# Even and odd tokens in the Hyena transforms, and the order of the work around them

## The reference

```
h   = modulated rmsnorm(x)                                  # 256 x 1024
u   = short_conv(h @ w_hyena)                               # 256 x 1536, cut into v, g1, g2 of 512
z   = v
for o in 0, 1:                                              # long convolution by FFT, then a gate
    z = g[o] * irfft(rfft(z, 512) * rfft(filter[o], 512))[:256]
q, k, v = h @ w_qkv (k and v also of 256 memory rows)       # 4 heads, rotary positions on q and k
a   = softmax(q1 k1) v - lambda * softmax(q2 k2) v          # differential attention, 8 (head, tile) pairs
x   = x + w_out(gates of h) . (z, norm(a));  x = x + swiglu(x)
```

## Time and profile before

| | |
|---|---|
| median of 3 runs | 1320.81 us (1318.42 to 1324.71) |
| profiled execution, its own time | 1318.56 us |
| its span | 1316.8 us |
| TensorE (PE) busy | 1278.4 us, 97% of the span |
| VectorE (DVE) busy | 695.5 us, 53% |
| ScalarE (ACT) busy | 500.4 us, 38% |
| granted TensorE clock, mean over the span | 0.999 |
| DMA | 363.15 MB, mean 276 GB/s |

### The profile page before, as it was taken

How to read it: one execution, slowest core, us unless ns; L and a number is a source line. 1 busy time by engine, 2 the same in 40 slices (tenths; PEclk the granted TensorE clock), 3 DMA queues, 4 the chain that set the end, 5 groups by cost and what they waited for, 6 DMA issues and landing times.

```text
span 1316.8 us, 17834 instructions
## 1 busy us (share of the span) xinstructions
PE 1278.4 (97%) x7078; PEld 892.6 (68%) x7078; DVE 695.5 (53%) x1192; ACT 500.4 (38%) x766; POOL 77.8 (6%) x86
## 2 busy tenths in 40 slices
PE   8999999999999999999999999999999999999998
PEld 7987886976675454444444444449957687799986
DVE  5675678667564322223222222257875877755552
ACT  5556574345332111111111111146414685744442
POOL 5740200100000000000000000000000000000000
PEclk9999999999999999999999999999999999999999
DMA  9654747959855999999999999995505235655540
GB/s 351 232 189 151 240 144 286 353 186 333 312 203 217 401 429 428 427 429 426 428 428 428 428 427 427 426 389 185 179 13 210 110 137 159 194 165 180 190 160 33
DMA packets 102100, 363.15 MB, mean 276 GB/s; under 512 B 4114, under 2 KB 28949, under 8 KB 89920
## 3 DMA queue, kind: packets, MB, share of 16 engines
q1 hardware_dynamic: 98656, 352.86, 69.1%
q0 software_dynamic: 3168, 9.06, 2.1%
q10 hardware_dynamic: 192, 0.06, 0.0%
HBM read 360.91 MB, written 1.05 MB: 275 GB/s over the span
## 4 chain that ended last, share of the span: by engine, by line
PE 86%; DVE 6%; ACT 4%; issue 2%; DMA 1%; ACTq 0%; DVEq 0%
PE bank L532 38%; PE bank L925 16%; PE bank L943 8%; PE bank L902 5%; PE bank L1290 5%; PE bank L972 3%; DVE ring_parts L1338 2%; PE bank L854 1%; PE bank L933 1%; PE bank L1093 1%; PE bank L1082 1%; ACT ring_parts L2163 1%; PE bank L586 1%; DMA ring<-in_w_xkv 1%; PE bank L621 1%
## 5 line engine op out<-in xcount | busy, mean ns | idle before, releaser
L2163 ACT ACTIVATE ring_parts<-ring 128x1024 fp32r<-128x1024 f32 x234 | 242.6, 1057 | 226.5 <-PE bank L532 198.7
L1338 DVE TENSOR_TENSOR ring_parts<-ring,ring_parts 128x1024 fp32r<-128x1024 f32 x214 | 257.0, 1223 | 129.8 <-ACT ring_parts L2163 126.9
L532 PE MATMUL bank<-ring_parts,arena_parts 128*128 128x512 f32 x1056 | 271.8, 392 | 3.6 <-ACT ring_parts L2163 1.5
L532 PEld LDWEIGHTS bank<-ring_parts,arena_parts 128*128 128x128 f32 x1056 | 196.5, 188 | 48.7 <-ACT ring_parts L2163 2.9
L532 PE MATMUL bank<-arena_parts,ring_parts 128*128 128x256 f32 x1504 | 198.0, 284 | 2.2 <-DVE ring_parts L1338 1.2
L925 PE MATMUL bank<-ring,arena 128*64 128x512 f32 x432 | 190.6, 594 | 9.1 <-issue 9.1
L926 PE MATMUL bank<-ring,arena 128*64 128x512 f32 x448 | 198.0, 595 | 0.0
L532 PEld LDWEIGHTS bank<-arena_parts,ring_parts 128*128 128x128 f32 x1504 | 190.1, 192 | 4.1 <-issue 2.7
L925 PEld LDWEIGHTS bank<-ring,arena 128*64 128x64 f32 x432 | 57.4, 137 | 127.6 <-issue 127.6
L532 PE MATMUL bank<-ring_parts 128*128 128x512 f32 (+1 forms) x624 | 117.1, 345 | 2.1 <-DVE ring_parts L1338 1.2
L532 PEld LDWEIGHTS bank<-ring_parts 128*128 128x128 f32 x624 | 96.6, 190 | 22.0 <-issue 7.1
(11 more groups left out here) (390 smaller groups left out, 1416.2 us busy)
## 6 DMA issues: line engine op xcount, KB each, us to landing
ring<-in_w SPq DMA_DIRECT2D x81, 2048.0 KB, 21.5
ring<-in_w_in SPq DMA_DIRECT2D x27, 2048.0 KB, 9.6
flank<-in_w SPq DMA_DIRECT2D x13, 2048.0 KB, 22.1
ring<-in_w_ada SPq DMA_DIRECT2D x12, 2048.0 KB, 8.7
ring<-in_w_ffn_gate SPq DMA_DIRECT2D x11, 1024.0 KB, 5.4
ring<-in_w_ffn_up SPq DMA_DIRECT2D x11, 1024.0 KB, 8.0
ring<-in_w_ffn_down SPq DMA_DIRECT2D x5, 2048.0 KB, 7.7
ring<-in_w_xkv SPq DMA_DIRECT2D x4, 2048.0 KB, 16.4
```

Source lines behind the costliest of these rows:

```text
L532: mm = pe.matmul(ps[:, o:o + width], *pair, start=(o == 0 and kk == 0 and ha + hw == 0), stop=(kk == kn - 1 and (ha, hw) == terms[-1] and ...
L1338: dve.tensor_tensor(low, src, high, ALU.subtract).then_inc(low_ready, 1)
L2163: act.activation(high, src, ACT.Copy).then_inc(high_ready, 1)
```

## The change

Tokens are taken as even and odd ones. The frequencies come in pairs whose tables differ in nothing but the sign of the odd tokens' part, so half of the products suffice and VectorE makes the two halves by a sum and a difference. This holds for the spectra, the forward transforms and, with sum and difference ahead of the product, for the way back. What is done on which engine:

- TensorE: `transformed(o)` is 4 fp32 products of 128x512 instead of 8, `convolved(o)` 4 instead of 8, the spectra 8 instead of 16 in all. Transposes and tables read every second token.
- ScalarE: a new `even_halves(o)` copies two of the four U banks to SBUF, since VectorE's sums read one operand from PSUM and one from SBUF.
- VectorE: `filtered(o)` is 4 operations on 512 elements from PSUM, then 6 on 1024 and 4 on 512 in SBUF, instead of 12 on 512. `spectra_of_halves` adds two operations of 1024 elements in each of the expert steps 2 and 3. `rotate(Kall)` is cut into its two tiles, with `split_low(2)` between; `rotate(Q)` still stands between the two orders.
- Fillers: `transformed(0)` follows the transposes directly, all four quarters of Q stand between it and `convolved(0)`, and all four of V between `transformed(1)` and `convolved(1)`. From there each filler is taken one place earlier: quarter 0 of p7 stands ahead of the attention loop, and its iterations use quarters 1 to 3 of p7, p8, and quarter 0 of p9. The calls of `split_low`, `split_high` and `gate_columns` follow.
- The input table of transforms is laid out anew, with the same number of DMAs.

The diff, cut to its core and its indentation by eight (edits of other tables' layouts are left out):

```
 add(name, *[((lambda u, i=i: u[:, 512 * i:512 * i + 512].rearrange("p (k n) -> p k n", k=2)),
-             w["dft"][i].rearrange("(k p) n -> p k n", p=P)) for i in range(4)])
+             w["dft"][i].rearrange("(p k) n -> p k n", k=2)) for i in range(2)],
+    *[((lambda u, i=i: u[:, 512 * i:512 * i + N]), w["dft"][i][0:P, :]) for i in (2, 3)])
 ...
+evens, Yother = [actT[:].rearrange("p k n -> p (k n)")[:, D * i:D * (i + 1)].rearrange("p (i n) -> p i n", i=2) for i in range(2)]
...
         ps = take(f"spec{o}{part}{f}", bank)
-        for t in range(NT):
-            mm = pe.matmul(ps[:], tab[:, t, f * P:(f + 1) * P], hF[:, t, (2 * o + part) * 512:(2 * o + part + 1) * 512],
-                           start=(t == 0), stop=(t == 1))
-        give(f"spec{o}{part}{f}", mm)
+        give(f"spec{o}{part}{f}", pe.matmul(ps[:], tab[:, f, 0:P], hF[:, f, (2 * o + part) * 512:(2 * o + part + 1) * 512],
+                                            start=True, stop=True))
...
             for j in range(4):
-                mm = pe.transpose(ps[:, j * P:(j + 1) * P], uT[:, 4 * i + j, t * P:(t + 1) * P], ident[:])
+                mm = pe.transpose(ps[:, j * P:(j + 1) * P], uT[:, 4 * i + j, t:N:2], ident[:])
...
     def transformed(o):
-        fcos, fsin = unit("dftB", 2, N, 0), unit("dftB", 2, N, 512)
-        if o:
-            pe.wait_ge(s["Z_ready"], 2)
-        else:
-            emptied(pe, "utok00", "utok10")
-        for part, tab in enumerate((fcos, fsin)):
-            for f in range(2):
-                ps = bank(f"U{o}{part}{f}")
-                for t in range(NT):
-                    mm = pe.matmul(ps[:], tab[:, t, f * P:(f + 1) * P], (Z if o else UT)[:, t, 0:DHY], start=(t == 0), stop=(t == 1))
-                give(f"U{o}{part}{f}", mm)
+        tabs = unit("dftB", 2, N, 0), unit("dftB", 2, N, 512)
+        for parity in range(2):
+            if o:
+                pe.wait_ge(s["Z_ready"], parity + 1)
+            else:
+                emptied(pe, f"utok{parity}0")
+            for part in range(2):
+                ps = bank(f"U{o}{part}{parity}")
+                give(f"U{o}{part}{parity}", pe.matmul(ps[:], tabs[part][:, parity, 0:P], (Z if o else UT)[:, parity, 0:DHY],
+                                                      start=True, stop=True))
     def convolved(o):
-        icos, isin = unit("dftB", 2, N, 1024), unit("dftB", 2, N, 1536)
-        pe.wait_ge(s["Y_ready"], 4 * (o + 1))
-        for t in range(NT):
-            ps = bank(f"conv{o}{t}")
-            n = 0
-            for tab, Y in ((icos, Yre), (isin, Yim)):
-                for f in range(2):
-                    mm = pe.matmul(ps[:], tab[:, f, t * P:(t + 1) * P], Y[:, f, :], start=(n == 0), stop=(n == 3))
-                    n += 1
-            give(f"conv{o}{t}", mm)
+        tabs = unit("dftB", 1, N, 1024), unit("dftB", 1, N, 1536)
+        for parity in range(2):
+            pe.wait_ge(s["Y_ready"], 2 * o + parity + 1)
+            ps = bank(f"conv{o}{parity}")
+            for part, Y in enumerate((Yre, Yother)):
+                mm = pe.matmul(ps[:], tabs[part][:, 0, parity:N:2], Y[:, parity, :], start=(part == 0), stop=(part == 1))
+            give(f"conv{o}{parity}", mm)
         if o:
             used("dftB")
-    filler("p3", 0, 1)
     transformed(0)
-    filler("p3", 2, 3)
+    filler("p3", 0, 1, 2, 3)
     convolved(0)
-    filler("p5", 0)
     transformed(1)
-    filler("p5", 1, 2, 3)
+    filler("p5", 0, 1, 2, 3)
     convolved(1)
     filler("p6", 0, 1)
     pe.wait_ge(s["Z_ready"], 4)
...
         for h in range(H):
             mm = pe.transpose(ps[:, h * P:(h + 1) * P], Q[:, t, h * P:(h + 1) * P], ident[:])
         give(f"qT{t}", mm)
-    filler("p6", 2)
+    filler("p6", 2, 3)
     for t in range(4):
         ps = bank(f"kT{t}")
         for h in range(H):
             mm = pe.transpose(ps[:, h * P:(h + 1) * P], Kall[:, t, h * P:(h + 1) * P], ident[:])
         give(f"kT{t}", mm)
-    filler("p6", 3)
+    filler("p7", 0)
     emptied(pe, *jobs_of("qT", 2), *jobs_of("kT", 4))
     def dscores(n):
...
     for n in range(H * NT):
         if n + 1 < H * NT:
             dscores(n + 1)
-        filler(("p7", "p8")[n // 4], n % 4)
+        filler(("p7", "p8", "p9")[(n + 1) // 4], (n + 1) % 4)
         turned_weights(n)
         if n:
             attended(n - 1)
-    filler("p9", 0)
+    filler("p9", 1)
     attended(H * NT - 1)
-    filler("p9", 1, 2, 3)
+    filler("p9", 2, 3)
     UNIT_END[SLOT["hT"]] = PART_END[-1]
     for q in range(4):
         place = 4 * hT_place + q
...
         dve.scalar_tensor_tensor(out=yB[1][:, c], in0=PS[4 + half][:], scalar=slot_gate, in1=yB[0][:, c],
                                  op0=ALU.mult, op1=ALU.subtract).then_inc(moe[f"low{half}"], 1)
+    def spectra_of_halves(o):
+        emptied(dve, *[f"spec{o}{part}{f}" for part in range(2) for f in range(2)])
+        even, odd = spectra[:, 0, o], spectra[:, 1, o]
+        did(dve.tensor_tensor(even, even, odd, ALU.add))
+        did(dve.scalar_tensor_tensor(out=odd, in0=odd, scalar=-2.0, in1=even, op0=ALU.mult, op1=ALU.add))
     def acc(n):
         for half in range(2):
             for t in range(NT):
...
             xg(n + 1, 1)
         low(n, 0)
         low(n, 1)
+        if n in (2, 3):
+            spectra_of_halves(n - 2)
         if not before:
             acc(n)
...
         did(dve.tensor_copy(UT[:, t, 0:512], ps[:]), free(f"utok{t}0"))
     emptied(dve, "p4_0", "p4_1")
     dve.wait_ge(s["rope_in"], 32)
-    rotate(Kall)
+    rotate(Kall, (0,))
     split_low(2)
     def filtered(o):
         hr, hi = spectra[:, :, o, 0, :], spectra[:, :, o, 1, :]
-        for f in range(2):
-            ur = full(dve, f"U{o}0{f}")
-            did(dve.tensor_tensor(Yre[:, f, :], ur[:], hr[:, f, :], ALU.mult), hold=False)
-            did(dve.tensor_tensor(Yim[:, f, :], ur[:], hi[:, f, :], ALU.mult), free(f"U{o}0{f}"), hold=False)
-        for f in range(2):
-            ui = full(dve, f"U{o}1{f}")
-            did(dve.tensor_tensor(Ytmp[:, f, :], ui[:], hi[:, f, :], ALU.mult))
-            did(dve.tensor_tensor(Yre[:, f, :], Yre[:, f, :], Ytmp[:, f, :], ALU.subtract), s["Y_ready"])
-            did(dve.tensor_tensor(Ytmp[:, f, :], ui[:], hr[:, f, :], ALU.mult), free(f"U{o}1{f}"))
-            did(dve.tensor_tensor(Yim[:, f, :], Yim[:, f, :], Ytmp[:, f, :], ALU.add), s["Y_ready"])
-    def gated_on(o):
+        for part, X in enumerate((Yre, Yim)):
+            emptied(dve, f"U{o}{part}0")
+            odd = full(dve, f"U{o}{part}1")
+            did(dve.tensor_tensor(X[:, 0, :], evens[:, part, :], odd[:], ALU.add), hold=False)
+            did(dve.tensor_tensor(X[:, 1, :], evens[:, part, :], odd[:], ALU.subtract), free(f"U{o}{part}1"))
+        did(dve.tensor_tensor(Ytmp, Yre, hr, ALU.mult), hold=False)
+        did(dve.tensor_tensor(Yother, Yim, hi, ALU.mult))
+        did(dve.tensor_tensor(Ytmp, Ytmp, Yother, ALU.subtract))
+        did(dve.tensor_tensor(Yother, Yre, hi, ALU.mult))
+        did(dve.tensor_tensor(Yim, Yim, hr, ALU.mult), hold=False)
+        did(dve.tensor_tensor(Yre[:, 0, :], Ytmp[:, 0, :], Ytmp[:, 1, :], ALU.add), hold=False)
+        did(dve.tensor_tensor(Yre[:, 1, :], Ytmp[:, 0, :], Ytmp[:, 1, :], ALU.subtract))
+        did(dve.tensor_tensor(Yim, Yim, Yother, ALU.add))
+        did(dve.tensor_tensor(Yother[:, 0, :], Yim[:, 0, :], Yim[:, 1, :], ALU.add), s["Y_ready"])
+        did(dve.tensor_tensor(Yother[:, 1, :], Yim[:, 0, :], Yim[:, 1, :], ALU.subtract), s["Y_ready"])
+    def gated_on(o, t):
+        emptied(dve, f"utok{t}{o + 1}")
+        ps = full(dve, f"conv{o}{t}")
+        did(dve.tensor_tensor(Z[:, t, :], ps[:], UT[:, t, (o + 1) * 512:(o + 2) * 512], ALU.mult), free(f"conv{o}{t}"))
+        dve.sem_inc(s["Z_ready"], 1)
+    rotate(Kall, (1,))
+    for o in range(2):
+        filtered(o)
         for t in range(NT):
-            emptied(dve, f"utok{t}{o + 1}")
-            ps = full(dve, f"conv{o}{t}")
-            did(dve.tensor_tensor(Z[:, t, :], ps[:], UT[:, t, (o + 1) * 512:(o + 2) * 512], ALU.mult), free(f"conv{o}{t}"))
-            dve.sem_inc(s["Z_ready"], 1)
-    filtered(0)
-    split_low(1)
-    gated_on(0)
-    split_low(3)
-    emptied(dve, "p3_0", "p3_1")
-    rotate(Q)
-    filtered(1)
-    split_low(2)
-    gated_on(1)
+            split_low(1)
+            gated_on(o, t)
+        if o == 0:
+            split_low(2)
+            emptied(dve, "p3_0", "p3_1")
+            rotate(Q)
     split_low(1)
     def tile_places(k):
         return [(slice(None), slice(0, 4), slice(t * P, (t + 1) * P)) for t in range(NT)]
-    split_banks(["zT0", "zT1"], zT_parts, tile_places(4))
-    split_low(2)
+    split_banks(["zT0", "zT1"], zT_parts, [(slice(None), slice(0, 4), slice(t, N, 2)) for t in range(NT)])
+    split_low(3)
     def columns(n):
         o = 8 + 8 * (n % 2)
...
     evicted("p5c", Vall, NT)
     split_high(4 * 3 + 2)
     evicted("p4", Kall)
+    def even_halves(o):
```

(14 more changed lines are left out.)

8 lines of the change are left out of this document (4 added, 4 removed).

## The result

The changed kernel takes 1345.07 us (median of 4 runs, 1343.07 to 1345.68), the kernel before 1321.1 us in the same comparison. The ratio is 1.0177, with a 95% interval of 1.015 to 1.0204: slower by 24 us, where 14 were forecast and the range ended at 1341. The profiled execution took 1344.96 us, its span 1343.2.

A forecast was written before the change was run, and what follows sets the result against it. TensorE, 97% busy, was taken as the bound, with the experts' stream DMA-bound. Spectra -2.3, loop with Hyena +14.8 and clock +1.7 made +14.2: 1332.8 on the profiled execution, 1335.0 us as median, range 1327 to 1341.

The forecast's parts named there:

- Part 1, the spectra: Ahead of the experts: halved spectra let the expert weight stream start earlier, taken as 2.3 us gained.
- That is 1.8 at the first place freed and 2.6 at the second: Gain in us when TensorE's expert products free places for the waiting weight queue; 2.3 was taken.
- whatever TensorE gains ahead of that is carried to the end: Expert stage: time gained before the weight queue resumes at 424.36 is kept, since the stream behind is DMA-bound.
- rival list: A forecast 0.78; B no Hyena waits 0.07; C loop not longer 0.04; D faster 0.04; E clock falls 0.07.
- Part 2, Hyena: Transforms and convolutions: 13.7 us of products removed, waits of 2.9, 3.1 and 6.1 us, leaving 2.0 us gained.
- Part 3, the bank of p7: Ahead of the loop: p7's quarter 0 waits 3.3 us for bank 6; scores start 4.1 us later.
- Part 4, the loop: Attention loop: low parts join one chain, period 7.3 us; +14.8 us overall, including Hyena's and the pre-loop gains and waits.
- Part 5, the tail: O's scaling and transposes stay covered by fillers, one quarter fewer (-2.7); separately, clock at the second convolution +1.7 us.
- rival E: TensorE's clock falls in several waits, so products and quarters behind them run at half speed: +6 us, 1341; chance 0.07.

The follow-up runs named there:

- ScalarE's two edits: The changed kernel with u's evictions ahead of the even-half copies and the first gate columns evicted ahead of K's transposes: 1346.57 us, ratio 1.0198.
- Both undoings: The changed kernel with ScalarE's high part ahead of exponentials(n+1): 1331.65 us; the changed kernel with K-transpose and loop fillers at their earlier places: 1326.53 us.

## Why the prediction was wrong

Its direction, and the mechanisms of four of its five parts, were right; the time lay 4 us above its range because of the first part. With that stage as forecast it would have been about 1336.

- **Part 1, the spectra (-2.3 forecast, +6.5 measured): failed, twice.** "That is 1.8 at the first place freed and 2.6 at the second" left out the clock: TensorE, with less to do ahead of the routing, waits 2.6 us at L882, and its clock falls. Window 410:415 of the changed kernel, and its chain:

```profile
410.00:415.00 5.00, 5.00 (x26) 3.84 (x26) 1.36 (x8) 1.09 (x2) 0.00 (x0) 0.66 0.40 167
```

```profile
410.47 1.87 PE bank L855 x2
412.33 4.25 PE bank L902 x32
416.58 0.86 PE bank L855 x2
```

  and the chain of before at the same place:

```profile
410.21 1.80 PE bank L854 x4
412.01 3.57 PE bank L902 x32
```

  Half of spectrum 5 takes 1.87 us where the whole took 1.80, and L902 takes 0.7 more; spectrum 6 gives its 0.86. On the time axis the queue resumes at 424.57 against 424.36. This execution had come to the stage 0.7 us late (the transposes ahead of all spectra, L588, at 388.90 against 388.16), so that some 0.5 was gained at the first place freed. At the end of the experts the changed kernel is ahead by 1.2 us, which is within what that place moves from one kernel to the next with nothing changed ahead of it.
  Then "whatever TensorE gains ahead of that is carried to the end" failed: the block of TensorE's instructions came in 881:882 instead of 872:873, and the stage lost 5.9 us of waiting and 1.9 on the low clock behind it (0.69 as the mean of 885:890). That the number of instructions ahead of the place decides is shown from both sides, by adding it back (with and without work: -4.6 and -5.3 us, 2 and 4 by the ratios, and the wait gone from the trace) and by taking it from the kernel before (+5.2). That it acts by the block's coming late is inferred, from the block's time in all seventeen traces. My rival list had no such case; no row that I had read spoke of instructions as something that has to be loaded, although the profile's page has them as a queue of their own.
- **Part 2, Hyena.** The waits were 2.2, 1.8 and 6.1 us for 2.9, 3.1 and 6.1. The stage came out at +1.0 instead of -0.3, mostly by the clock: the second convolution lost 2.7 us (6.16 for 3.44), where I had taken 1.7, and VectorE's chain up to it was 0.3 longer than worked out. The clock fell behind the first wait too, which I had ruled out: it is 0.84 in 965:970, and Q's four quarters take 12.6 us for 10.9. That cost no time, since VectorE ended last there; it only made the wait ahead of the first convolution shorter. That VectorE's list is what ends last is shown by Q's late rotation, and by ScalarE's two edits, which took the wait ahead of the fourth transform product away and only made the next one longer.
- **Part 3, the bank of p7.** 3.2 us for 3.3.
- **Part 4, the loop.** +14.5 for +13.4, period 7.24 for 7.3. Both undoings, of the order on ScalarE and of the shift, brought the time back, 13.4 and 18.5 us.
- **Part 5, the tail.** -2.7 as forecast.
- **The clock, rival E.** It had 0.07 and against it the argument that no row showed a fall behind a wait of 2 to 3 us. In the changed kernel there are such rows: 0.66 in 410:415 behind a wait of 2.6 us, and 0.84 in 965:970 behind one of 2.2. The trace agrees with the rule of the Trainium skill that the prediction names ("TensorE: Matmul & The Clock Gate", section "HAM oscillation — how this bites in real kernels"), that bursts of products with waits between them get throttled. The loop ran at 0.91 as the mean of 1030:1050 too, but there the price was nothing, since VectorE set the pace. Where it had a price is the second convolution (2.7 us), the routing (0.8) and the stretch behind the late block (1.9).

What stays open: why the block is late. The step between 16 and 24 instructions suggests that its request hangs on a place in TensorE's list, which no run shows by itself; and the end of the experts is a place where TensorE's list stops at four waits in a row and the DMA engines are full; which of the two makes it late was not tried. Why the spread of the experts' end is 3.7 us between kernels with the same list up to there is open too.
